# Gate and up projections of a hybrid decoder block: sixteen tiles as seven half-size matrix products

## Chip, cores and metric

One NeuronCore of a Trainium2 chip runs the whole program. The metric is device time in microseconds, the median of several runs; "span" is the time from the first to the last instruction in one profiled execution. TensorE is the matmul engine, VectorE, ScalarE and GpSimd are the three elementwise engines, SyncE only issues DMAs here.

## What is computed

The reference is one layer of a decoder block on x (1 x 512 x 1024, float32). Cut to what matters:

```
h = rms_norm(x, norm1); proj = h @ w_in
... differential attention (4 heads), native sparse attention (8 heads) ...
x = x + concat([o_diff, o_nsa]) @ w_out
h = rms_norm(x, norm2)
x = x + (silu(h @ w_gate) * (h @ w_up)) @ w_down        # w_gate, w_up: 1024 x 2816, w_down: 2816 x 1024
return rms_norm(x, final_norm)
```

## The kernel before

**Three matmuls for one.** Every float32 operand is split in two halves of fewer bits, high and low, and a product is the sum of high*high, high*low and low*high. A weight chunk (512 KB, 128 x 1024) goes through a ring: SyncE loads it into one of 3 `raw` slots, ScalarE rounds it to `w_hi` (one of 4 slots), and `w_lo` = `raw` - `w_hi` is made by GpSimd (`split`) for all chunks up to the down projection, and by VectorE (`split_down`) for those of the down projection. SyncE loads chunk k only when the low half of chunk k-3 is made; ScalarE makes the high half of chunk k only when TensorE is done with chunk k-4. Each queue works strictly in its written order.

**Stages.** Until about 312 us of the profiled execution: norm, input projection, attention and output projection, woven together by a written order of slots and jobs. There are 38 weight chunks in it; number 30 to 37 are those of the output projection (jobs `og` and `od`). The differential heads need each key half on both halves of the partitions: `double_keys` on GpSimd's queue copies them with four DMAs a head.

Then 22 tiles f of 128 hidden columns (`columns`): 24 matmuls of 512 columns for gate, 24 for up, on the un-normalised, transposed x (`xT_hi`, `xT_lo`: 8 blocks of 128 features by 512 tokens). VectorE takes each result from PSUM and multiplies it with the token's inverse norm `norm_b` (`gate_n`, `up_n`), ScalarE applies silu, VectorE multiplies. TensorE may start on a bank again when VectorE has taken it two tiles before (`s_gn`, `s_un`).

Last, the down projection as seven products of half matrices in place of eight (Strassen's method in Winograd's form, indices A11 to A22 and S1 to S4 for the token and feature halves and their sums, T1 to T4 for the weight sums). The seven combinations `form` of the hidden tiles are made by VectorE after every second tile. The four weight sums are made in DRAM: SyncE copies a piece (`down_sums`), and an accumulating DMA on GpSimd's queue (`add_sum`) adds the other; 24 such jobs of 256 to 512 KB, one behind each chunk from the fifth of gate and up on. A GpSimd job waits for its copy and for the accumulation four jobs before it, and the splits behind it in GpSimd's queue wait with it.

Of the kernel before, what the change touches and what calls it, by code (L numbers as in the profile page):

```python
# [25 lines left out]
P = 128  # L26
D = 1024
# [97 lines left out]

SUMS = [(T1, (0, 1), ("w", 0, 0)), (T3, (0, 1), ("w", 1, 1)), (T2, (0, 0), ("sum", T3)), (T4, (1, 0), ("sum", T2))]
SUM_AT = 4


def tiles_of(g):  # L130

    return 2 * g, min(2 * g + 2, FP)


def plan_chunks():
# [42 lines left out]
def hymba_block(nc, x, norm1, w_in, lambda_q1, lambda_k1, lambda_q2, lambda_k2, diff_subln,  # L178
# [8 lines left out]
    job_of = {c: j for j, c in enumerate(jobs)}  # L187

# [115 lines left out]
    with ExitStack() as ctx:  # L304
# [29 lines left out]
        with ExitStack() as compress:  # L334

            blk = [sb(f"blk{i}", [P, 16, 2, GROUPS * NC], F32R, compress) for i in range(2)]
        xres = sb("xres", [P, NT, D])
        with ExitStack() as second:

            high1 = sb("high1", [P, FP, HALF], F32R, second)  # L340
# [34 lines left out]
        with ExitStack() as swiglu:  # L375
            with ExitStack() as full:

                form = sb("form", [P, N_PROD, FP, HALF], F32, full)
            form_lo = sb("form_lo", [P, N_PROD, FP, HALF], F32R, swiglu)
            high0 = sb("high0", [P, FP, HALF], F32R, swiglu)  # L380
# [33 lines left out]
        s_last, s_gx = sem("s_last"), sem("s_gx")  # L414
        s_silu, s_prod, s_forms = sem("s_silu"), sem("s_prod"), sem("s_forms")
# [10 lines left out]
        HIGH = (high0, high1)  # L426
# [39 lines left out]
        def sum_job(i):  # L466

            to, begin, add = SUMS[i // GROUPS_M]
            return to, i % GROUPS_M, ("w",) + begin, add

        def sum_index(to, g):
            return [x_[0] for x_ in SUMS].index(to) * GROUPS_M + g

        def sum_done(eng, to, g):
            i = sum_index(to, g)
            eng.wait_ge(s_added[i % 4], 16 * (i // 4 + 1))

# [33 lines left out]
        def chunk_cols(k):  # L511
            if chunks[k][0] == "down":
                m0, m1 = tiles_of(chunks[k][1][1])
                return 512 * (m1 - m0)
            return SLOT if chunks[k][0] == "vg" else 1024

        def low_done(eng, k):

            if k >= down0:
                eng.wait_ge(s_dlo, k - down0 + 1)  # L520
            else:
                eng.wait_ge(s_split, k + 1)
# [14 lines left out]
        def _(sp):  # L537
# [9 lines left out]
            for k in range(len(chunks)):  # L547
# [11 lines left out]
                if chunks[k][0] == "vg":  # L559
# [5 lines left out]
                    sp.dma_start(dst[:, :, P:V_COLS], w[:, :, COL["vw"]:COL["gt"] + GATES]).then_inc(signal, 16)  # L565
# [1139 lines left out]
```

## Time and profile before

| what | value |
|---|---|
| median of 3 runs | 676.9 us (673.18 to 677.26) |
| the profiled execution | 673.63 us |
| its span | 671.8 us |
| granted TensorE clock, mean | 0.998 of full speed |
| TensorE matmul, busy | 659.1 us of the span |
| VectorE, ScalarE, GpSimd busy | 382.0, 321.9, 253.8 us |
| moved by DMA | 100.33 MB |

Busy matmul time overlaps from one matmul to the next, so its share says that TensorE has work, not at what rate; the rate is read from start to start. Waits are read per engine and per stage, since the stages have different limits.

### The profile page before, as it was taken

To read this page: it belongs to the slowest core of one execution; us is meant where nothing else is said; L and a number is where in the kernel's file an instruction comes from. 1 tells how busy PE (TensorE), PEld (TensorE's weight loads), DVE (VectorE), ACT (ScalarE), POOL (GpSimd) and SP (SyncE) were. 2 spreads that over 40 slices of the span, in tenths; PEclk is the share of its full clock that TensorE was granted. 3 is DMA by queue.
4 is the path that set the end of the run, shared out by engine and by line. 5 is a ranking of instruction groups with operands and counts; after the bars stand their busy time and mean duration, and the time that the engine had idled before them with its cause. 6 is when DMAs were issued, how large, how long until landed. Compare 5 with 4: busy or idle time off the path is not lost.

```text
span 671.8 us, 9932 instructions
## 1 busy us (share of the span) xinstructions
PE 659.1 (98%) x3483; PEld 558.8 (83%) x3483; DVE 382.0 (57%) x860; ACT 321.9 (48%) x658; POOL 253.8 (38%) x148
## 2 busy tenths in 40 slices
PE   9999999999999998999999999999999999999996
PEld 7988988898899887888788888888888888888884
DVE  6445356555665687523494466543444155778794
ACT  7546456688554477534432222222222224656663
POOL 4752242691212040222385576755444410000132
PEclk9999999999999999999999999999999999999999
DMA  8764341576222031223499999997333323766653
GB/s 252 201 141 125 88 120 49 153 188 215 54 59 63 17 80 16 63 64 95 156 230 296 277 267 282 302 271 176 94 101 96 107 80 128 204 179 198 186 172 127
DMA packets 103007, 100.33 MB, mean 149 GB/s; under 512 B 4036, under 2 KB 76848, under 8 KB 102960
## 3 DMA queue, kind: packets, MB, share of 16 engines
q1 hardware_dynamic: 93048, 83.23, 40.9%
q0 software_dynamic: 7776, 14.06, 11.7%
q10 hardware_dynamic: 2136, 2.43, 1.3%
q8 instruction: 28, 0.46, 0.3%
q14 instruction: 19, 0.16, 0.1%
HBM read 95.49 MB, written 27.54 MB: 183 GB/s over the span
## 4 chain that ended last, share of the span: by engine, by line
PE 93%; DVE 2%; issue 2%; POOL 1%; ACT 1%; POOLq 0%; DVEq 0%; ACTq 0%
PE bank L685 16%; PE bank L687 16%; PE bank L686 16%; PE bank L666 9%; PE bank L668 9%; PE bank L667 9%; PE bank L838 5%; PE bank L814 3%; PE bank L798 2%; PE bank L799 2%; PE bank L877 1%; PE bank L680 1%; POOL w_lo L619 1%; PE bank L832 1%; PE bank L851 1%
## 5 line engine op out<-in xcount | busy, mean ns | idle before, releaser
L619 POOL TENSOR_TENSOR w_lo<-raw,w_hi 128x1024 fp32r<-128x1024 f32 (+1 forms) x82 | 202.7, 2481 | 291.5 <-ACT w_hi L1006 290.8
L1006 ACT CAST w_hi<-raw 128x1024 fp32r<-128x1024 f32 (+2 forms) x123 | 125.4, 1025 | 202.9 <-PE bank L687 73.3
L685 PE MATMUL bank<-xT_hi,w_hi 128*128 128x512 f32 x464 | 184.0, 397 | 1.0 <-POOL w_lo L619 0.7
L687 PE MATMUL bank<-xT_hi,w_lo 128*128 128x512 f32 x464 | 182.4, 393 | 0.0
L686 PE MATMUL bank<-xT_lo,w_hi 128*128 128x512 f32 x464 | 182.0, 392 | 0.0
L687 PEld LDWEIGHTS bank<-xT_hi,w_lo 128*128 128x128 f32 x464 | 87.2, 188 | 19.7
L685 PEld LDWEIGHTS bank<-xT_hi,w_hi 128*128 128x128 f32 x464 | 87.3, 188 | 19.5 <-issue 1.1
L686 PEld LDWEIGHTS bank<-xT_lo,w_hi 128*128 128x128 f32 x464 | 87.4, 188 | 17.9 <-issue 0.2
L1431 DVE CUSTOM_DVE_ANT_0 bank<-bank,bias 128x128 f32<-128x128 f32 (+3 forms) x96 | 47.6, 497 | 75.8 <-PE bank L799 46.2
L668 PE MATMUL bank<-w_hi,form_lo 128*128 128x512 f32 x154 | 60.7, 394 | 0.0
L666 PE MATMUL bank<-w_hi,high 128*128 128x512 f32 x154 | 60.5, 393 | 0.0
L667 PE MATMUL bank<-w_lo,high 128*128 128x512 f32 x154 | 60.5, 393 | 0.0
L1087 ACT ACTIVATE E<-bank,nmax 128x128 f32<-128x128 f32 (+3 forms) x80 | 42.4, 531 | 35.7 <-DVE nmax L1431 34.8
L1588 DVE TENSOR_TENSOR w_lo<-raw,w_hi 128x1024 fp32r<-128x1024 f32 (+1 forms) x42 | 48.9, 1171 | 17.7 <-ACT w_hi L1006 17.4
L659 POOL TENSOR_TENSOR xres<-xres,final_g 128x512 f32<-128x512 f32 x7 | 13.0, 1879 | 111.5 <-ACT gate_n L1012 111.5
L1625 DVE TENSOR_TENSOR up_n<-bank,norm_b 128x512 f32<-128x512 f32 x22 | 15.1, 689 | 70.2 <-PE bank L687 70.2
L1099 ACT COPY PT<-bank 128x384 f32<-128x384 f32 (+3 forms) x84 | 35.4, 422 | 28.4 <-PE bank L814 28.0
L838 PEld LDWEIGHTS bank<-v_nsa,PT 128*128 128x128 f32 x320 | 43.5, 191 | 4.7 <-issue 1.6
L838 PE MATMUL bank<-v_nsa,PT 128*128 128x64 f32 x320 | 43.2, 266 | 0.3 <-DVE mix L1494 0.2
L814 PE MATMUL bank<-ident,E 128*128 128x128 f32 x208 | 36.8, 274 | 0.0
L1621 DVE TENSOR_TENSOR gate_n<-bank,norm_b 128x512 f32<-128x512 f32 x22 | 15.1, 688 | 35.4 <-PE bank L687 30.2
L667 PEld LDWEIGHTS bank<-w_lo,high 128*128 128x128 f32 x154 | 28.9, 188 | 6.7
(205 smaller groups left out, 1081.7 us busy)
## 6 DMA issues: line engine op xcount, KB each, us to landing
raw<-in_w_gate_dram SPq DMA_DIRECT2D x22, 512.0 KB, 8.1
raw<-in_w_up_dram SPq DMA_DIRECT2D x22, 512.0 KB, 6.8
raw<-in_w_in_dram SPq DMA_DIRECT2D x20, 512.0 KB, 4.3
down_sums<-in_w_down_dram SPq DMA_DIRECT2D x20, 512.0 KB, 12.4
raw<-down_sums SPq DMA_DIRECT2D x20, 512.0 KB, 3.8
raw<-in_w_down_dram SPq DMA_DIRECT2D x15, 512.0 KB, 3.5
down_sums<-in_w_down_dram POOLq DMA_DIRECT2D x10, 512.0 KB, 9.5
down_sums<-down_sums POOLq DMA_DIRECT2D x10, 512.0 KB, 8.9
```

Of the source, the lines that this page charges most:

```text
L619: nc.gpsimd.tensor_tensor(wv_lo(k)[:, 0:n], raw[:, k % RAW_SLOTS, 0:n], wv_hi(k)[:, 0:n].bitcast(F32), ALU.subtract).then_inc(s_split, 1)
L666: nc.tensor.matmul(o, a_hi, b_hi, start=first, stop=False)
L667: nc.tensor.matmul(o, a_hi, b_lo, start=False, stop=False)
L668: return nc.tensor.matmul(o, a_lo, b_hi, start=False, stop=last)
L685: nc.tensor.matmul(bank[:, :], hi, xT_hi[:, kt, :], start=kt == 0, stop=False)
L686: nc.tensor.matmul(bank[:, :], hi, xT_lo[:, kt, :], start=False, stop=False)
L687: return nc.tensor.matmul(bank[:, :], lo, xT_hi[:, kt, :], start=False, stop=kt == KT - 1)
L814: mm = nc.tensor.transpose(TURN[n % 2][:, j * P:(j + 1) * P], E[:, s % E_SLOTS, j * P:(j + 1) * P], ident[:, :])
L838: mm = nc.tensor.matmul(bank[:, 0:v.shape[1]], PT[:, n % 2, j * P:(j + 1) * P], v, start=j == 0, stop=j == i)
L1006: nc.scalar.copy(wv_hi(k)[:, 0:n], raw[:, k % RAW_SLOTS, 0:n]).then_inc(s_whi, 1)
L1431: nc.vector.tensor_tensor_reduce(out=bank[:, 0:n], in0=bank[:, 0:n], in1=bias[:, m % BIAS_SLOTS, 512 - n:512], scale=1.0, scalar=3.0e38, o ...
L1588: nc.vector.tensor_tensor(wv_lo(k)[:, 0:n], raw[:, k % RAW_SLOTS, 0:n], wv_hi(k)[:, 0:n].bitcast(F32), ALU.subtract).then_inc(s_dlo, 1)
```

## The change

The first six tiles (F0 = 6) stay as they are. For tiles 6 to 21 gate and up together are one 512 x 1024 times 1024 x 256 product: the token halves and the feature halves of x are the left side, gate's and up's columns, each with two feature halves, the right side. It is done as seven products of half matrices: a tile has 7 x 4 x 3 = 84 matmuls of 256 columns in place of 48 of 512. Its weights come in four chunks of 512, 512, 512 and 256 KB (`mixed`, c = 0 to 3), each of two loads of 256 KB (the last of one).

- The weight sums T1 to T4 of w_gate and w_up are made in DRAM (`mixed_sums`), in 32 more jobs of 512 KB copy and 512 KB accumulation. All 56 jobs are placed anew: ten behind chunks 6 to 15, ten behind 27 to 31, twelve behind 34 to 37, then twelve of the down sums behind the first twelve chunks of gate and up, and twelve behind every fifth of the mixed chunks.
- During tiles 0 to 5 VectorE also makes the normalised x (`normal_columns`: an addition of two SBUF tiles and a multiplication with PSUM for each of 8 blocks), four sums of its quarters (`x_sum`, 1024 columns) and the low halves of the seven left sides (`x_low`, 1024 columns); ScalarE makes their high halves (`x_high`).
- In the mixed tiles VectorE combines the seven results (seven additions of 256 columns, with ScalarE copying the first from PSUM), and VectorE, not GpSimd, makes the low halves of chunks c = 0 and 2. The product with silu of tile f-1 (`swiglu_tile`) stands in VectorE's order between the first addition of tile f and the low half of chunk (f+1, 0).
- The residual x is saved to DRAM after the output projection, since its space is taken, and loaded back in four pieces of 512 KB (`BACK`) in the down projection.
- `double_keys` has two DMAs a head in place of four.
- The down projection's six groups of tiles are 2, 2, 2, 1, 2, 2 in place of 2, 2, 2, 2, 2, 1.

```diff
+F0 = 6
+UNITS = [(A11, ("w", 0, 0)), (A12, ("w", 1, 0)), (S2, ("sum", T2)), (S3, ("sum", T3)),
+         (S1, ("sum", T1)), (A22, ("sum", T4)), (S4, ("w", 1, 1))]
+N_UNIT = 4
+X_ORDER = [A11, A12, S2, S3, A22, S1, S4]
+WIDE = 4
+BACK = {(0, 5): (0, 0), (1, 1): (0, 1), (1, 3): (1, 1), (2, 1): (1, 0)}
+X_FULL = {0: (0, 1, 2), 1: (3, 4, 5), 2: (6, 7)}
+X_SUMS = {2: (0, 1), 3: (2, 3)}
+X_SPLIT = {3: (A11, A12), 4: (S2, S3, A22), 5: (S1, S4)}
...
-    for f in range(FT):
+    for f in range(F0):
         chunks += [("gate", f), ("up", f)]
+    for f in range(F0, FT):
+        chunks += [("mixed", (f, c)) for c in range(N_UNIT)]
...
+    sum_at = [6 + i for i in range(10)] + [27 + i // 2 for i in range(10)] + [34 + i // 3 for i in range(12)]
+    sum_at += [n_fill + i for i in range(12)] + [n_fill + 2 * F0 + 2 + 5 * i for i in range(12)]
+    by_dve = [c[0] == "down" or (c[0] == "mixed" and c[1][1] in (0, 2)) for c in chunks]
...
-                    for z in range(2):
-                        k_ = k_diff[:, jobs[j][1] % 2, z, hd, :]
-                        pool.dma_start(k_[there, :], k_[here, :]).then_inc(s_dup[jobs[j][1]], 16)
+                    k_ = k_diff[:, jobs[j][1] % 2, :, hd, :]
+                    pool.dma_start(k_[there, :, :], k_[here, :, :]).then_inc(s_dup[jobs[j][1]], 16)
...
+            for f in range(F0, FT):
+                pe.wait_ge(s_un, f - 1)
+                for c in range(N_UNIT):
+                    k = index[("mixed", (f, c))]
+                    low_done(pe, k)
+                    for z, j in enumerate(units_of(c)):
+                        a = UNITS[j][0]
+                        if f == F0:
+                            pe.wait_ge(s_xlo, X_ORDER.index(a) + 1)
+                        o = SET[f % 2][c][:, HALF * z:HALF * z + HALF]
+                        for kt in range(4):
+                            w = slice(512 * z + P * kt, 512 * z + P * kt + P)
+                            nc.tensor.matmul(o, wv_hi(k)[:, w], x_hi(a)[:, kt, :], start=kt == 0, stop=False)
+                            nc.tensor.matmul(o, wv_hi(k)[:, w], x_lo(a)[:, kt, :], start=False, stop=False)
+                            mm = nc.tensor.matmul(o, wv_lo(k)[:, w], x_hi(a)[:, kt, :], start=False, stop=kt == 3)
+                    mm.then_inc(s_chunk, 1)
...
+            def normal_columns(kt):
+                x_ = x_full[:, kt, :]
+                link(nc.vector.tensor_tensor(x_, xT_hi[:, kt, :].bitcast(F32), xT_lo[:, kt, :].bitcast(F32), ALU.add))
+                nc.vector.tensor_tensor(x_, x_, NORM_BANK[:, :], ALU.mult).then_inc(s_xfull, 1)
...
+            for f in range(F0, FT):
+                first, second_, third, fourth = SET[f % 2]
...
+                dve.wait_ge(s_chunk, chunk[0])
+                dve.wait_ge(s_first, f - F0 + 1)
+                dve.wait_ge(s_prod, f - 1)
+                nc.vector.tensor_tensor(gate_[:, early], first_p, first[:, late_], ALU.add)
+                if f > F0:
+                    swiglu_tile(f - 1)
+                split_own(index[("mixed", (f, 0))] + SPLIT_SLOTS)
+                dve.wait_ge(s_chunk, chunk[1])
+                link(nc.vector.tensor_tensor(run_u, first_p, second_[:, early], ALU.add))
+                link(nc.vector.tensor_tensor(run_v, run_u, second_[:, late_], ALU.add))
+                split_own(index[("mixed", (f, 1))] + SPLIT_SLOTS)
+                dve.wait_ge(s_chunk, chunk[2])
+                dve.wait_ge(s_forms, f // 2)
+                nc.vector.tensor_tensor(gate_[:, late_], run_v, third[:, late_], ALU.add).then_inc(s_gn, 1)
+                nc.vector.tensor_tensor(up_[:, late_], third[:, early], run_v, ALU.subtract)
+                split_own(index[("mixed", (f, 2))] + SPLIT_SLOTS)
+                dve.wait_ge(s_chunk, chunk[3])
+                link(nc.vector.tensor_tensor(up_[:, early], fourth[:, early], run_u, ALU.subtract))
+                nc.vector.tensor_tensor(up_[:, early], up_[:, early], third[:, early], ALU.add).then_inc(s_un, 1)
+                split_own(index[("mixed", (f, 3))] + SPLIT_SLOTS)
+            swiglu_tile(FT - 1)
```

## Rows read from the trace of the kernel before

**Rows 1.** The page: busy time of the engines, and the chain that ended last

```profile
PE 659.1 (98%) x3483; PEld 558.8 (83%) x3483; DVE 382.0 (57%) x860; ACT 321.9 (48%) x658; POOL 253.8 (38%) x148
...
PE 93%; DVE 2%; issue 2%; POOL 1%; ACT 1%; POOLq 0%; DVEq 0%; ACTq 0%
```

**Rows 2.** Busy time by window, gate and up without sum jobs

```profile
470.00:555.00 85.00, 85.00 (x371) 69.45 (x370) 35.42 (x54) 22.61 (x28) 32.39 (x13) 1.00 0.33 98
```

**Rows 3.** Timeline of VectorE, up results of tiles 15 and 20: start, duration

```profile
492.62 0.69 DVE L1625 TENSOR_TENSOR up_n<-bank,norm_b 128x512 f32<-128x512 f32 x1 [4.77 <-PE bank L687]
...
547.86 0.69 DVE L1625 TENSOR_TENSOR up_n<-bank,norm_b 128x512 f32<-128x512 f32 x1 [4.77 <-PE bank L687]
```

**Rows 4.** Timeline of TensorE, 256 columns back to back, 22 starts apart

```profile
205.09 0.28 PE L667 MATMUL bank<-w_lo,xT_hi 128*128 128x256 f32 x1
...
207.71 0.28 PE L668 MATMUL bank<-w_hi,xT_lo 128*128 128x256 f32 x1
```

**Rows 5.** The page, costliest groups: halves of the weights

```profile
L619 POOL TENSOR_TENSOR w_lo<-raw,w_hi 128x1024 fp32r<-128x1024 f32 (+1 forms) x82 | 202.7, 2481 | 291.5 <-ACT w_hi L1006 290.8
L1006 ACT CAST w_hi<-raw 128x1024 fp32r<-128x1024 f32 (+2 forms) x123 | 125.4, 1025 | 202.9 <-PE bank L687 73.3
```

**Rows 6.** VectorE's groups by form, 470 to 555 us

```profile
L1636 DVE TENSOR_TENSOR form<-up_n,form 128x256 f32<-128x256 f32 x4 | 10.0, 2508 | 0.1
L1625 DVE TENSOR_TENSOR up_n<-bank,norm_b 128x512 f32<-128x512 f32 x8 | 5.5, 692 | 38.1 <-PE bank L687 38.1
...
L1588 DVE TENSOR_TENSOR w_lo<-raw,w_hi 128x1024 fp32r<-128x1024 f32 x2 | 2.4, 1217 | 0.0
...
L1638 DVE TENSOR_TENSOR form<-form 128x256 f32<-128x256 f32 x4 | 1.7, 417 | 0.0
```

**Rows 7.** Timeline of GpSimd at 493 us

```profile
493.81 2.57 POOL L619 TENSOR_TENSOR w_lo<-raw,w_hi 128x1024 fp32r<-128x1024 f32 x1 [3.05 <-ACT w_hi L1006]
```

**Rows 8.** Timeline of VectorE at 494 us

```profile
494.15 2.51 DVE L1636 TENSOR_TENSOR form<-up_n,form 128x256 f32<-128x256 f32 x1
```

**Rows 9.** Timeline of VectorE, tiles 0 and 1

```profile
333.13 0.69 DVE L1621 TENSOR_TENSOR gate_n<-bank,norm_b 128x512 f32<-128x512 f32 x1 [5.18 <-ACT norm_b L1213]
...
337.97 0.69 DVE L1625 TENSOR_TENSOR up_n<-bank,norm_b 128x512 f32<-128x512 f32 x1 [0.22 <-PE bank L687]
339.18 8.35 DVE L1633 TENSOR_TENSOR form<-gate_n,up_n 128x256 f32<-128x256 f32 x1 [0.51 <-ACT gate_n L1223]
```

**Rows 10.** Timeline of GpSimd, splits and sum jobs of the same time

```profile
337.25 2.88 POOL L619 TENSOR_TENSOR w_lo<-raw,w_hi 128x1024 fp32r<-128x1024 f32 x1
339.61 1.66 POOL L638 DMA_DIRECT2D down_sums<-in_w_down_dram  x1
...
343.48 3.76 POOL L619 TENSOR_TENSOR w_lo<-raw,w_hi 128x1024 fp32r<-128x1024 f32 x1
```

**Rows 11.** DMA, 470 to 555 us, no sum jobs: share of 16 engines, us to landing

```profile
q1 hardware_dynamic: 12706, 8.30, 32.4%
...
raw<-in_w_gate_dram SPq DMA_DIRECT2D x5, 512.0 KB, 3.9
```

**Rows 12.** DMA issues, 345 to 450 us, a sum job behind each load

```profile
down_sums<-in_w_down_dram SPq DMA_DIRECT2D x15, 512.0 KB, 12.5
raw<-in_w_gate_dram SPq DMA_DIRECT2D x10, 512.0 KB, 11.6
```

**Rows 13.** DMA issues, 320 to 345 us, where the sum jobs begin

```profile
raw<-in_w_up_dram SPq DMA_DIRECT2D x3, 512.0 KB, 4.3
raw<-in_w_gate_dram SPq DMA_DIRECT2D x2, 512.0 KB, 7.1
```

**Rows 14.** Timeline of GpSimd, output projection: splits of chunks 36 and 37

```profile
289.09 4.77 POOL L619 TENSOR_TENSOR w_lo<-raw,w_hi 128x1024 fp32r<-128x1024 f32 x2 [8.40 <-ACT w_hi L1006]
```

**Rows 15.** Timeline of TensorE: first use of chunk 37

```profile
302.37 0.40 PE L666 MATMUL bank<-w_hi,mixT 128*128 128x512 f32 x1
```

**Rows 16.** Timeline of TensorE: the matmul behind the key-doubling DMAs at 129 us

```profile
129.40 0.47 PE L685 MATMUL bank<-xT_hi,w_hi 128*128 128x512 f32 x1 [0.72 <-POOL w_lo L619]
```

More of the change, by code:

```diff
@@ L464, in part, with mixed_part, sum_part, sum_done @@
             return w[:, m0:m1, rows_, 512 * dh:512 * dh + 512]
[L466 to L475, printed above, removed]
+        def mixed_part(what, f0, n, k0=0, n_k=4):
+            if what[0] == "sum":
+                w = mixed_sums[what[1]].rearrange("(k p) n -> p k n", p=P)
+                return w[:, k0:k0 + n_k, P * (f0 - F0):P * (f0 - F0 + n)]
+            rows_, up = what[1:]
+            w = (w_up if up else w_gate)[0].rearrange("(k p) n -> p k n", p=P)
+            return w[:, 4 * rows_ + k0:4 * rows_ + k0 + n_k, P * f0:P * (f0 + n)]
+        def sum_part(i, what):
+            kind, _, at_, _, _ = todo[i]
+            if kind == "down":
+                return part(what, at_[0])
+            return mixed_part(what, F0 + WIDE * at_[0], WIDE, 2 * at_[1], 2)
+        def sum_done(eng, kind, to, at_):
+            i = [x_[:3] for x_ in todo].index((kind, to, at_))
             eng.wait_ge(s_added[i % 4], 16 * (i // 4 + 1))
+        def units_of(c):
+            return range(2 * c, min(2 * c + 2, len(UNITS)))
         def chunk_src(k):
@@ L514, in chunk_cols @@
                 return 512 * (m1 - m0)
+            if chunks[k][0] == "mixed":
+                return 512 * len(units_of(chunks[k][1][1]))
             return SLOT if chunks[k][0] == "vg" else 1024
         def low_done(eng, k):
[L519 to L522, printed above, removed]
+            eng.wait_ge(s_dlo if by_dve[k] else s_split, sum(by_dve[m] == by_dve[k] for m in range(k + 1)))
         SHARE = OUTP[(len(turned) - 1) % 2][:, 256:512]
@@ L588, in _ @@
                 sp.wait_ge(s_y, t + 1)
[L589 removed]
+                sp.dma_start(out[0, t * P:(t + 1) * P, 0:c], xlast[:, t, 0:c]).then_inc(s_out, 16)
             sp.wait_ge(s_out, 16 * (NT + 1))
@@ L599, in raw_landed @@
         def raw_landed(eng, k):
-            loads = sum(2 if chunks[m][0] == "vg" else 1 for m in range(k % RAW_SLOTS, k + 1, RAW_SLOTS))
+            loads = sum(2 if chunks[m][0] == "vg" or chunks[m][0] == "mixed" and len(units_of(chunks[m][1][1])) > 1 else 1
+                        for m in range(k % RAW_SLOTS, k + 1, RAW_SLOTS))
             eng.wait_ge(s_raw[k % RAW_SLOTS], 16 * loads)
@@ L1618, in _, with split_own @@
+            def split_own(k):
+                if k < len(chunks) and by_dve[k]:
+                    split_down(k)
+            for f in range(F0):
                 dve.wait_ge(s_chunk, late(("gate", f)))
```

247 lines of the change are left out of this document (182 added, 65 removed).

## The prediction

> **What bounds the kernel now.** I read the page first: TensorE is busy for 659.1 of 671.8 us and holds 93% of the chain that ended last [rows 1]. Then the windows: between 470 and 555 us it is busy all 85 us, at the higher of its two clock levels (granted clock 1.00, 2.4 GHz), while VectorE is busy 35 and GpSimd 32 us [rows 2]. So gate and up are bound by the number of matmuls times their spacing. The spacing I take from starts: the up results of tiles 15 and 20 are fetched 55.24 us apart, so a tile takes 11.05 us, and with 48 matmuls that is 0.230 us each [rows 3]. The duration printed for a matmul is of no use here, since neighbours overlap.
>
> **What the change removes.** 84 matmuls of 256 columns replace 48 of 512. The same shape stands back to back in the attention part: 22 intervals in 2.62 us, 0.1191 us each, at the full clock, with another weight block before each, as in the new loop [rows 4]. A mixed tile is then 84 x 0.1191 = 10.00 us, 1.05 less than before. Sixteen tiles: **16.7 us** is what there is to gain, 2.5% of the span. (Half the width costs 0.52 of the full one, so seven eighths of the columns become 0.905 of the time.) All else that the change does must hide behind TensorE, and for each I name the cover.
>
> **Weights through the ring.** A tile's weights grow from 1 MB in 11.05 us to 1.75 MB in 10.0 us. A raw slot sees all four kinds of chunk in three tiles. Outside the load it is held for three whole and one half high parts (3 x 1.03 + 0.6 = 3.7 us), and for the low parts: two by VectorE at 1.22, one and a half by GpSimd at 2.48, together 6.2 us [rows 5, 6]. With a load time L that is (4L + 9.9)/3 per tile. With L = 3.9 us, as without sum jobs [rows 11], it gives 8.5 us, below TensorE's 10.0. It reaches 10.0 us at L = 5.0, and the old 11.05 at L = 5.8. What L will be is open: without other traffic 1 MB in 11.05 us took 32.4% of the DMA engines [rows 11], so 1.75 MB in 10.0 us take about 0.63. One sum job follows every fifth chunk, every 12.5 us; before there was one every 5.5 us, and L was 11.6 [rows 12]. Where the jobs began, loads took 4.3, and those caught with a copy 7.1 us [rows 13]. If two in five are caught, L is 5.4 on average, but a chunk is needed only when TensorE has used up what is split: four high and low slots, 10 us of work, so that one late load is absorbed. Bounds: nothing, to (4 x 5.8 + 9.9)/3 = 11.05, the whole gain. I take 1 us, near the lower end, because the late ones come singly.
>
> **VectorE against GpSimd.** This is where I expect most of the loss. A VectorE operation on two SBUF tiles takes 0.417 us at 256 columns, and the same operation directly behind the start of a GpSimd split takes 2.51 us [rows 6, 8]. The split runs from 493.81 to 496.38, the VectorE operation ends at 496.66 [rows 7, 8]: it waited for the split to end. Results from PSUM (0.692 us for 512 columns) don't show it [rows 6]. At tile 1, with GpSimd at splits and sum jobs one after another, a single operation took 8.35 us [rows 9, 10]. Before, VectorE had time for that. Now there are two places where it has not.
>
> First, **tiles 0 to 5**. VectorE starts at 333.8 us with the new work [rows 9]. On two SBUF tiles: 8 additions of 512 columns (0.68 each, between 0.417 and 1.217), four sums and seven low halves of 1024 (11 x 1.22), 27 products and combinations of 256 (0.417 each), two low halves of weights (1.22 each) [rows 6], 32.6 us in all. From PSUM: 8 multiplications and 12 results, 20 x 0.69 = 13.8 us. GpSimd makes nine and a half low parts in that time, 23.6 us [rows 5]. If all PSUM work runs under GpSimd's, S1's low half is ready 32.6 + 23.6 - 1.2 = 55.0 us after 333.8, at 388.8; if none does, at 402.6. TensorE wants it two chunks into tile 6: tile 1 ends at 337.9 [rows 9], four more tiles to 382.1, and 48 matmuls, 387.8 us. So this costs between 1 and 15 us, once. I take 6: about two thirds of the PSUM work finds a split to run under.
>
> Second, **the mixed tiles**. TensorE can't begin tile f+1 before VectorE has made the low half of chunk (f+1, 0), whose slot is free when chunk (f, 0) is done. From then: ScalarE's high half 1.05, its copy of the first result and VectorE's first addition 0.4 each, `swiglu_tile`, the low half 1.22 us. With an even f-1 `swiglu_tile` has two operations, 0.8 us, and all is done after some 4.1 us. With an odd f-1 it has seven, 2.9 us: 6.2 us with the handovers. TensorE has three chunks, 60 x 0.1191 = 7.15 us of cover. But GpSimd begins (f+1, 1) after 2.86 + 1.05 + 0.1 = 4.0 us, in the midst of the seven, and holds VectorE back until 6.5: the low half is there after 8.4 us, and TensorE waits 1.2 us. Every second tile, 8 x 1.2 = 9.6 us at most. It is nothing where GpSimd's chunk lands 0.6 us later, since then VectorE's low half is under way first. I take half, 5 us.
>
> **Attention and output projection.** 32 sum jobs lie here. SyncE and GpSimd wait in them, and the splits behind wait too. In the attention part low halves are made long before use. The tight place is twelve jobs behind chunks 34 to 37. The splits of 36 and 37 ended at 293.9 [rows 14]. Chunk 37 is first used at 302.4 us [rows 15], so it has 8.5 us of cover. Two jobs in front of it wait for sums four or eight jobs earlier, each some 9 to 12 us from issue to landing under load (the copy took 12.5, [rows 12]); laid out one after the other this puts its split at about 301.5. It costs 0 to 3 us; I take 0.5. The two fewer key DMAs a head can give at most what TensorE waited behind that queue, 0.72 us at 129 us [rows 16]; I take 0.5. The save and reload of the residual, four loads of 512 KB in the down projection, each come three or more chunks before use: 0, unless the ring there, now with 14% more loads, runs late. The changed groups: 0.
>
> **Sum.** 16.7 + 0.5 - 6 - 5 - 1 - 0.5 = 4.7 us. On the profiled execution (673.6 us, span and 1.8 around it) that is 668.9. The median of the runs is 3.3 us higher, so on the median's footing **672 us**.
>
> **The rivals.**
> (a) All is hidden. For it: in the old trace TensorE never waits in this stage, and where VectorE lags the queues shift by themselves until the collisions stop. Then 16.7 + 0.7 less the 1 us that can't be avoided: 660 us.
> (b) VectorE sets the pace of the mixed tiles. Its work a tile is seven combinations (2.9), two low halves (2.4) and on average 4.5 operations of `swiglu_tile` (1.9), 7.3 us, and GpSimd's 3.7 us beside it; if they exclude each other wholly, 11.0 us a tile, and the gain is gone while the 6 us before tile 6 stay: 682 us. Against it: the seven combinations read PSUM.
> (c) Slower: the weight ring. If one load in four takes 11.6 us, as under steady sum jobs, and the others 4.3 [rows 12, 13], L is 6.1 and a tile takes 11.4 us; 0.35 x 16 = 5.7 us lost, plus 6 before tile 6: 688 us. It decides from L = 5.8 on. For it: every such load passes through SyncE's one queue with the copies. Against it: a sum job only every 12.5 us.
> (d) Half the columns don't give half the time. The rows give 0.1191 against 0.230 us [rows 3, 4], so 0.01. The Trainium skill, "TensorE: Matmul & The Clock Gate", section "Back-to-back issue gap", states about 81 ns for 128 and 131 ns for 512 columns in a sustained stream; read between the two, 256 columns would cost some 98 ns, 84 of them 8.2 us against 6.3 us for 48 of the old, and the change would lose 1.9 us a tile by that estimate, about 707 us. This case's trace doesn't agree with either figure: its 512 columns stand 230 ns apart.
>
> The other place where a page bears on it: the Trainium skill, "DMA: Bandwidth & Descriptors", section "Measured (HBM→SBUF, 128 partitions, SWDGE, issued from GpSimd)", advises transfers of 1 MiB and more and lists 138 GB/s at 64 KB and 341 GB/s at 1 MB, and the change cuts its loads from 512 to 256 KB. By it each load would be less efficient, which pushes towards (c). The two of a chunk follow each other in one queue, so I count them as one of 512 KB.
>
> **Chances.** The forecast (most of the gain eaten by waits, 665 to 679) 0.46, (a) 0.22, (b) 0.16, (c) 0.15, (d) 0.01. A measurement tells about 1% here, 6.8 us. Below 670.1 lie (a) and four tenths of the forecast: 0.41. Within lie the rest of it and half of (b): 0.35. Above 683.7 the rest, 0.24. The range of 8 in 10 takes in (a) nearly whole and (b), and about half of (c): 661 to 687 us.
>
> **What the new profile would show.** Matmuls of 256 columns 0.119 us apart inside a chunk. A wait of TensorE for `x_lo` or for the low half before the third chunk of tile 6, with VectorE operations of 0.4 to 1.2 us stretched to 3 before it. From tile 7 on a wait of about 1 us before the first matmul of every second tile, put down to VectorE's `w_lo`. Loads of 256 KB in the mixed stage with a median under 5 us; if TensorE's waits there are put down to GpSimd's low halves, and ScalarE's to the loads, (c) is right. A wait at the output projection's last chunk of up to 3 us. The prediction is wrong on the fast side if VectorE's operations stretch less than here because GpSimd has less to do, and on the slow side if loads stay above 5.8 us.

## The result, and the profile after

The changed kernel takes **727.1 us** (median of 4 runs, 725.9 to 728.9) against 676.7 us of before: ratio 1.076, 95% interval [1.072, 1.080]. I had forecast 672 us, 661 to 687. The page of the profiled execution (728.9 us, span 727.1):

```profile
PE 662.8 (91%) x4059; PEld 589.4 (81%) x4059; DVE 455.2 (63%) x999; ACT 357.9 (49%) x713; POOL 272.6 (37%) x172
...
q1 hardware_dynamic: 128696, 114.69, 51.4%
q0 software_dynamic: 16352, 30.84, 24.4%
...
PE 47%; DMA 19%; issue 13%; POOL 9%; DVE 7%; ACT 3%; SPq 1%; POOLq 0%; DVEq 0%; ACTq 0%
```

TensorE has only 3.7 us more busy time than before, but its share of the chain that ended last fell from 93% [rows 1] to 47%; DMA transfers hold 19%. Three marks of the timelines say where the 55.3 us of span went. VectorE's first use of `norm_b` comes at 358.65 us, 25.5 later than before [rows 9]. Tile 5 ends 25.9 us later than before (408.0 against 382.1), so tiles 0 to 5 lose hardly more. The mixed stage then lasts from 408.0 to 614.0 us, 206 us where sixteen old tiles took 16 x 11.05 = 176.8 [rows 3]: 29.2 more. What follows is as long as before, within 0.3 us.

```profile
358.65 0.69 DVE L1835 TENSOR_TENSOR gate_n<-bank,norm_b 128x512 f32<-128x512 f32 x1 [3.96 <-ACT norm_b L1346]
```

**Loss 1, 25.5 us before `norm_b`.** TensorE's waits in the output projection and behind it, and busy time by window (TensorE's is the second number; behind the engines stand the granted clock, the DMA engines' share and GB/s):

```profile
302.83 0.49 PE L781 MATMUL bank<-w_hi,mixT 128*128 128x512 f32 x1 [3.33 <-POOL w_lo L733]
335.62 0.79 PE L800 MATMUL bank<-xT_hi,w_hi 128*128 128x512 f32 x1 [12.57 <-DVE xT_lo L1490]
```

```profile
300.00:320.00 20.00, 17.17 (x76) 14.15 (x77) 5.42 (x8) 4.31 (x10) 11.36 (x9) 0.91 1.11 219
320.00:340.00 20.00, 7.43 (x24) 5.63 (x23) 3.92 (x6) 5.31 (x11) 7.54 (x5) 0.68 1.05 250
```

The first wait, 3.33 us, is for the low half of chunk 36. GpSimd's rows show its split and that of chunk 37, and TensorE's row the first use of chunk 37, which came just in time:

```profile
299.88 2.80 POOL L733 TENSOR_TENSOR w_lo<-raw,w_hi 128x1024 fp32r<-128x1024 f32 x1
...
309.55 2.85 POOL L733 TENSOR_TENSOR w_lo<-raw,w_hi 128x1024 fp32r<-128x1024 f32 x1
```

```profile
312.82 0.39 PE L781 MATMUL bank<-w_hi,mixT 128*128 128x512 f32 x1
```

Chunk 37 is used 10.5 us later than before [rows 15], ahead of the large wait. Of these, 3.8 us are there by 282.8 us, behind a wait for the key copies at 256.6. The profiled execution of **keys** below, which has no job more than the kernel before, is 3.1 us late at the same place, and that of **nomix** is not; so this part comes and goes between executions, and the jobs aren't shown to be its cause.

The sixteen DMA engines are full. The wait of 12.57 us is put down to VectorE's `xT_lo`, but that waited for ScalarE, and ScalarE for a load. ScalarE's row and SyncE's queue (start, time that the issue took) show why:

```profile
331.18 1.04 ACT L1139 CAST w_hi<-raw 128x1024 fp32r<-128x1024 f32 x1 [15.37 <-DMA raw<-in_w_up_dram]
```

```profile
302.71 0.37 SPq L677 DMA_DIRECT2D raw<-in_w_up_dram  x1
303.12 11.50 SPq L682 DMA_DIRECT2D down_sums<-in_w_down_dram  x1
314.67 2.77 SPq L677 DMA_DIRECT2D raw<-in_w_gate_dram  x1
317.48 14.48 SPq L682 DMA_DIRECT2D down_sums<-in_w_down_dram  x1
```

The load of chunk 39 (tile 0's `up`), issued at 302.71, landed at about 331, 28 us later. A copy for the sums kept SyncE for 11.50 and 14.48 us in the issue alone, with the next load behind it. ScalarE makes high halves in the order of the ring, so tile 0's late `up` weights held back the residual's high columns, which TensorE needed first.

**Loss 2, 29.2 us in the mixed stage, where 16.7 were to be gained.** The half-width matmuls are as forecast, 22 intervals in 2.64 us inside tile 6, 0.120 us each [rows 4]; then the waits begin:

```profile
408.10 0.28 PE L1097 MATMUL bank<-xa,w_hi 128*128 128x256 f32 x1
...
410.74 0.29 PE L1098 MATMUL bank<-xa,w_lo 128*128 128x256 f32 x1
...
421.86 0.55 PE L1096 MATMUL bank<-xs,w_hi 128*128 128x256 f32 x1 [6.11 <-DVE xs L1802]
422.21 0.41 PE L1097 MATMUL bank<-xs,w_hi 128*128 128x256 f32 x1
422.42 0.41 PE L1098 MATMUL bank<-xs,w_lo 128*128 128x256 f32 x1
```

Before tile 6's sums TensorE waits 7.7 us in all (1.64 and 6.11), and right behind the second wait the starts stand 0.21 us apart in place of 0.12, at the lower of the two clock levels; the window from 422 to 426 us (the clock is third from the end) has it at half:

```profile
422.00:426.00 4.00, 4.00 (x19) 4.00 (x20) 4.00 (x3) 0.00 (x0) 1.94 (x1) 0.50 0.01 2
```

Waits and lower clock together make tile 6 20.1 us long, 10.1 more than its 84 x 0.119. From there on, the list of waits between 425 and 610 us (in total, times, longest), and VectorE's first addition of each mixed tile (shortest, median, longest ns; first and last start):

```profile
DVE gate_n L1857 <- ACT sq L1387: 58.7, 14, 6.6
ACT w_hi L1139 <- DMA raw<-mixed_sums: 38.7, 26, 4.5
...
PE bank L1096 <- DVE w_lo L1753: 25.1, 11, 6.6
```

```profile
L1857 DVE TENSOR_TENSOR gate_n<-sq,bank x16: 406/421/424, 424.9 to 608.5; 128x256 f32<-128x256 f32 x16
```

Fifteen tiles in 183.6 us, **12.24 us a tile**. TensorE's own starts, from tile 7 to the first matmul of the down projection, give 12.40: 36.0 us over fifteen times 10.0, of which 25.1 are the waits above and some 8 are lost by matmuls that start 0.21 us apart behind them, at the lower clock. TensorE waits for VectorE's low halves, VectorE for ScalarE's copy of the first result (58.7 us in 14 times), and ScalarE, which rounds the next tile's first chunk ahead of that copy, for its load. The loads of 256 KB from the sums had a median of 4.8 us, those from `w_gate` 3.9. A chunk is two such loads (the last of a tile one); from the issue of its first to the landing of its last it took 5.35 us on the mean of all mixed chunks from tile 7 on.

### The profile page after: what moved, and what is told of

The parts are those of the page before. It is cut to its first block, busy times and chain, and to the rows that moved or that the text cites. A ratio compares the mean times of both kernels' runs of the same rounds, so it can differ in the third digit from the quotient of the medians.

```text
span 727.1 us, 11548 instructions
## 1 busy us (share of the span) xinstructions
PE 662.8 (91%) x4059; PEld 589.4 (81%) x4059; DVE 455.2 (63%) x999; ACT 357.9 (49%) x713; POOL 272.6 (37%) x172
## 3 DMA queue, kind: packets, MB, share of 16 engines
q1 hardware_dynamic: 128696, 114.69, 51.4%
q0 software_dynamic: 16352, 30.84, 24.4%
## 4 chain that ended last, share of the span: by engine, by line
PE 47%; DMA 19%; issue 13%; POOL 9%; DVE 7%; ACT 3%; SPq 1%; POOLq 0%; DVEq 0%; ACTq 0%
POOL w_lo L733 7%; PE bank L781 6%; PE bank L783 6%; PE bank L782 6%; DMA down_sums<-in_w_down_dram 6%; PE bank L953 4%; DMA raw<-mixed_sums 4%; DMA raw<-in_w_gate_dram 4%; PE bank L800 4%; PE bank L802 3%; PE bank L801 3%; PE bank L929 2%; DMA mixed_sums<-in_w_up_dram 2%; PE bank L913 2%; DVE w_lo L1753 2%
## 5 line engine op out<-in xcount | busy, mean ns | idle before, releaser
L1139 ACT CAST w_hi<-raw 128x1024 fp32r<-128x1024 f32 (+1 forms) x155 | 151.9, 985 | 201.4 <-DMA raw<-in_w_up_dram 63.5
L1753 DVE TENSOR_TENSOR w_lo<-raw,w_hi 128x1024 fp32r<-128x1024 f32 x74 | 90.2, 1219 | 25.5 <-ACT w_hi L1139 25.3
L800 PE MATMUL bank<-xT_hi,w_hi 128*128 128x512 f32 x208 | 84.8, 408 | 13.5 <-DVE xT_lo L1490 12.8
L802 PE MATMUL bank<-xT_hi,w_lo 128*128 128x512 f32 x208 | 82.7, 397 | 0.0
L801 PE MATMUL bank<-xT_lo,w_hi 128*128 128x512 f32 x208 | 82.6, 397 | 0.0
L1096 PE MATMUL bank<-xs,w_hi 128*128 128x256 f32 x256 | 73.6, 288 | 8.3 <-DVE xs L1802 7.7
L1097 PE MATMUL bank<-xs,w_hi 128*128 128x256 f32 x256 | 73.2, 286 | 0.0
L1098 PE MATMUL bank<-xs,w_lo 128*128 128x256 f32 x256 | 73.1, 286 | 0.0
L1096 PEld LDWEIGHTS bank<-xs,w_hi 128*128 128x128 f32 x256 | 49.9, 195 | 8.8 <-issue 8.1
L774 POOL TENSOR_TENSOR xlast<-xlast,final_g 128x512 f32<-128x512 f32 x7 | 12.8, 1851 | 101.1 <-ACT gate_n L1145 101.1
L1097 PEld LDWEIGHTS bank<-xs,w_hi 128*128 128x128 f32 x256 | 49.7, 194 | 0.0
L1098 PEld LDWEIGHTS bank<-xs,w_lo 128*128 128x128 f32 x256 | 49.6, 194 | 0.0
L802 PEld LDWEIGHTS bank<-xT_hi,w_lo 128*128 128x128 f32 x208 | 39.6, 191 | 9.2
L1857 DVE TENSOR_TENSOR gate_n<-sq,bank 128x256 f32<-128x256 f32 x16 | 6.7, 420 | 63.5 <-ACT sq L1387 58.7
## 6 DMA issues: line engine op xcount, KB each, us to landing
mixed_sums<-mixed_sums POOLq DMA_DIRECT2D x16, 512.0 KB, 12.4
```

The costliest lines, as they stand in the source:

```text
L800: nc.tensor.matmul(bank[:, :], hi, xT_hi[:, kt, :], start=kt == 0, stop=False)
L801: nc.tensor.matmul(bank[:, :], hi, xT_lo[:, kt, :], start=False, stop=False)
L802: return nc.tensor.matmul(bank[:, :], lo, xT_hi[:, kt, :], start=False, stop=kt == KT - 1)
L1096: nc.tensor.matmul(o, wv_hi(k)[:, w], x_hi(a)[:, kt, :], start=kt == 0, stop=False)
L1097: nc.tensor.matmul(o, wv_hi(k)[:, w], x_lo(a)[:, kt, :], start=False, stop=False)
L1098: mm = nc.tensor.matmul(o, wv_lo(k)[:, w], x_hi(a)[:, kt, :], start=False, stop=kt == 3)
```

## The experiments

Two theories. **A:** the sum jobs (a copy and an accumulate, DRAM to DRAM, 512 KB each) fill the DMA engines; loads come late. **B:** in the mixed tile the copy of the first result stands behind a load on ScalarE, which closes a loop. The main rival is that VectorE, slowed by GpSimd, or the order of the ring sets the pace whatever the loads take. Every time below is a median, and its ratio is to runs of the kernel before on the same chip (674.7 to 677.1 us there). The kernels named nomix leave the weight sums of gate and up out and load plain weights in their place, and those named nodown do the same with the twelve late down sums, so they compute another output.

**keys.** The key DMAs alone, in the kernel before: one DMA for both parts, `s_dup` at 32 in place of 64.

> The kernel before with two key-doubling DMAs a head in place of four, nothing else. Every theory: between 0 and 0.7 us faster than before, no change that a measurement tells; none of the 50 us comes from here.

674.4 us, 0.997 [0.995, 1.000]. TensorE's wait of 0.72 us at 129 us [rows 16] is now 0.5. The sign is right; the size, 2.7 us between the medians, is at the edge of what can be measured and more than this wait can give.

**nomix.** Theory A alone.

```diff
-    for wide in range(0, (FT - F0) // WIDE, 2):
+    for wide in ():
-  mixed_part(UNITS[j][1], f, 1)
+  mixed_part(("w", 0, 0) if UNITS[j][1][0] == "sum" else UNITS[j][1], f, 1)
```

> The changed kernel without its 32 jobs that make the weight sums of gate and up in DRAM (the loads of those sums take a piece of the gate weights in their place, so the results are not the reference's). Theory A (the early loss is the DMA engines filled with the twelve jobs behind chunks 34 to 37): the 25.9 us before tile 0's results are gone, norm_b is reached by 333 to 335 us, and the mixed stage stays at 12.9 us a tile: 699 to 704 us. Rival (GpSimd's waits in its own queue or ScalarE's order, not the engines' load, or the save of the residual): most of the 25.9 us stays, 720 us.

702.3 us, 1.039 [1.036, 1.041]; `norm_b` is used at 332.2 us. Loss 1 is gone, all of it, with the save of the residual still in place, so theory A holds for that stretch. The price of a job: the two large DMA queues' shares are 51.4 + 24.4% of 727.1 us after and 45.7 + 11.7% of 700.0 here, so 32 jobs took (551.1 - 401.8)/32 = **4.7 us of all sixteen engines each**. This is the time of their packets as the view counts it, which also gave windows shares of 1.11, so it is a price under load and no lower bound. The mixed tile is unchanged:

```profile
L1853 DVE TENSOR_TENSOR gate_n<-sq,bank x16: 407/421/422, 397.9 to 581.5; 128x256 f32<-128x256 f32 x16
```

**spread** and **spread_first.** The twelve jobs of chunks 34 to 37 go behind 32 and 33, the down jobs four chunks later; the second kernel also turns ScalarE's order round.

```diff
-    ... + [34 + i // 3 for i in range(12)]
+    ... + [32] * 4 + [33] * 8
```

```diff
 for c in range(N_UNIT):
-    weights_hi(index[("mixed", (f, c))] + SPLIT_SLOTS)
     if c == 0:
+        act.wait_ge(s_chunk, late(("mixed", (f, 0))))
         act.wait_ge(s_gn, f)
         nc.scalar.copy(first_p, SET[f % 2][0][:, 0:HALF]).then_inc(s_first, 1)
+    weights_hi(index[("mixed", (f, c))] + SPLIT_SLOTS)
```

> The changed kernel, all jobs kept, with the last twelve mixed jobs four behind chunk 32 and eight behind chunk 33 (where DMA engines and GpSimd are idle before 276 us) and the down jobs four chunks later, as the kernel before had them. Theory A: the jobs are done before the output projection's last chunks are loaded, and the time is as without the jobs, 699 to 706 us. Rival (it is the number of jobs and the load they put on the attention part, wherever they stand): no better than 720 us.

> As the kernel with the jobs moved, and in the mixed tiles ScalarE copies the first result out of PSUM before it makes the next high half, not behind it. Theory B (the mixed stage loses by order: VectorE's seven operations and the low half behind them stand behind ScalarE's copy, which stands behind a high half that waits for its load): VectorE's operations move into the time of the load, TensorE's 25 us of waits for the low half fall by half or more, 8 to 20 us faster than with the jobs moved alone. Theory C (the ring itself: load, high, low and the next load take longer than three chunks of TensorE, whatever the order): 0 to 4 us faster.

spread: 739.9 us, 1.093 [1.089, 1.098], a miss. GpSimd's and TensorE's rows:

```profile
270.01 1.14 POOL L751 DMA_DIRECT2D mixed_sums<-mixed_sums  x1 [2.31 <-DMA mixed_sums<-mixed_sums]
270.69 1.67 POOL L741 DMA_DIRECT2D k_diff<-k_diff  x2
```

```profile
281.31 0.45 PE L913 MATMUL bank<-k_diff,q_diff 128*128 128x128 f32 x1 [26.49 <-issue]
```

The last head's key DMAs were issued behind eight accumulates and took up to 9.9 us to land, the second at 281.2, and TensorE stood 26.5 us for those keys. spread_first: 718.0 us, 1.062 [1.059, 1.065]. Theory B holds, 22 us against spread (18 between the two profiled executions).

**first.** The changed kernel with ScalarE's order turned round and nothing else.

> The changed kernel, with one thing exchanged on ScalarE: in each of the sixteen mixed tiles it first copies the finished first product out of its bank, and then rounds the weights of the next tile's first chunk (before: the other way round, so that the copy stood behind a load that had not landed). Theory B (the stage lost its time to the copy behind a late load, which stopped VectorE, which holds the chunk that the next load waits for): the same 20 to 24 us as between the two kernels with their jobs elsewhere (739.9 and 718.0), so 703 to 707; VectorE's waits for ScalarE's copy fall from 58.7 us to under 10, the mixed stage takes about 11.7 us a tile. Rival (what was gained there belonged to the other place of the sum jobs): within 5 us of 727.

716.3 us, 1.058 [1.056, 1.061]: 10.8 us gained, half of what was expected, though VectorE's wait for the copy fell from 58.7 to 5.0 us and the tile to 11.15 us. Part of the contrast is in which executions are compared: between the profiled ones this pair differs by 14.7 us and the spread pair by 18.2. The order costs time here too; how much of the 22 us belonged to the other places of the jobs stays open.

**nomix_first**, **nomix_nodown**, **nomix_first_nodown.** With nomix these are the four corners: order of the copy, and the twelve down jobs inside the mixed stage. The second edit:

```diff
-    return todo
+    return todo[:-12]
-    sum_at = ... + [n_fill + 2 * F0 + 2 + 5 * i for i in range(12)]
+    sum_at = [n_fill + i for i in range(12)]
```

> Both known losses taken away: the 32 sum jobs of gate and up are left out (their loads read 256 KB of the gate weights in their place, so the output is another), and ScalarE copies the first result before it rounds the next weights. Theory (the two losses are independent and add up): 702.3 less 22 = 680, norm_b used at 332, 11.6 us a mixed tile. Rival (without the jobs the DMA engines are less full, so that the loads come sooner and the ring no longer sets the tile): 10.0 to 10.6 us a tile, 655 to 665.

> As the run without the 32 sum jobs of gate and up and with the copy of the first result first (688.7 us, 11.5 us a mixed tile), and also without the twelve jobs of the down sums that were issued inside the mixed stage (the loads of those sums read down weights in their place). Theory (the ring paces the tile by full DMA engines: 1.84 MB of weights a tile are 6.3 us of all sixteen at some 290 GB/s, and three quarters of a job at 4.5 us are 3.4 more, 9.7 of the 10.0 that TensorE needs): without them the median load falls from 5.3 to under 4.3 us and the tile to 10.0 to 10.4 us, 667 to 672. Rival (the order of work on ScalarE, VectorE and GpSimd in the ring sets it, whatever the loads take): 11.2 us a tile or more, 684 to 689.

> The changed kernel with its own order on ScalarE (the next tile's weights rounded ahead of the copy of the first result), without the 32 sum jobs of gate and up and without the twelve of the down sums inside the mixed stage (their loads read plain weights, so the output is another). With the copy first the same kernel took 666.6 us, 9.81 us a mixed tile. Theory (the order costs only because the loads come late behind full DMA engines): the loads land in time here, within 3 us of 666.6, 9.8 to 10.0 us a tile. Rival (the order is a cause of its own): 11 us a tile or more, 683 or more.

Without the 32 jobs, in us. A tile is given between VectorE's first additions, and by TensorE's starts from tile 7 on; a load as the median of one of 256 KB, and as the mean of a chunk from first issue to last landing:

```
                                  copy behind the load           copy first
12 jobs   time (ratio to before)  702.3 (1.039 [1.036, 1.041])   688.7 (1.019 [1.016, 1.023])
          a tile, both ways       12.24, 12.41                   11.50, 11.69
          one load; a chunk       4.8; 5.4                       5.3; 5.9
no job    time (ratio to before)  690.7 (1.024 [1.020, 1.027])   666.6 (0.988 [0.985, 0.991])
          a tile, both ways       11.37, 11.38                   9.81, 10.00
          one load; a chunk       3.9; 4.3                       4.3; 4.6
```

Each cause alone costs about two thirds of what both cost. nomix_first took 9 us more than its theory had (two losses that add up) and 24 more than the upper end of its rival; nomix_first_nodown is where its theory put it. With the jobs gone and the copy first, TensorE is busy 140 of 140 us; this is the stage as it was meant:

```profile
400.00:540.00 140.00, 140.00 (x1179) 140.00 (x1178) 101.38 (x191) 66.10 (x90) 54.60 (x27) 1.00 0.66 184
```

TensorE's first matmuls of tiles 8 and 21 stand thirteen tiles and 130.00 us apart, 10.00 us a tile:

```profile
411.03 0.28 PE L1094 MATMUL bank<-xa,w_hi 128*128 128x256 f32 x1
...
541.03 0.28 PE L1094 MATMUL bank<-xa,w_hi 128*128 128x256 f32 x1
```

The 9.81 from the additions is too low as a pace of TensorE: VectorE's first addition of tile 6 comes late, behind the entry, and the later ones catch up.

VectorE's additions of the two copy-first kernels, without and with the twelve jobs, and the issues of each between 400 and 550 us:

```profile
L1856 DVE TENSOR_TENSOR gate_n<-sq,bank x16: 407/421/422, 398.3 to 545.5; 128x256 f32<-128x256 f32 x16
```

```profile
q1 hardware_dynamic: 53070, 27.51, 64.9%
...
raw<-in_w_gate_dram SPq DMA_DIRECT2D x84, 256.0 KB, 4.3
```

```profile
L1854 DVE TENSOR_TENSOR gate_n<-sq,bank x16: 408/416/422, 398.5 to 571.0; 128x256 f32<-128x256 f32 x16
```

```profile
q1 hardware_dynamic: 49035, 27.85, 65.0%
q0 software_dynamic: 2464, 4.72, 19.2%
...
raw<-in_w_gate_dram SPq DMA_DIRECT2D x78, 256.0 KB, 5.3
```

A median load 1.0 us longer, or 1.3 us a chunk, costs 1.7 us a tile: the ring has no slack at 5.3. nomix_nodown refutes what I expected of it (that the order is harmless where loads are in time). Its loop, in ScalarE's, VectorE's and SyncE's rows:

```profile
474.47 1.05 ACT L1137 CAST w_hi<-raw 128x1024 fp32r<-128x1024 f32 x1 [0.68 <-DMA raw<-in_w_gate_dram]
475.43 0.36 ACT L1385 COPY sq<-bank 128x256 f32<-128x256 f32 x1
```

```profile
463.09 0.42 DVE L1855 TENSOR_TENSOR gate_n<-sq,bank 128x256 f32<-128x256 f32 x1 [3.27 <-ACT sq L1385]
...
465.81 2.61 DVE L1757 TENSOR_TENSOR form_lo_a<-form_a,high_a 128x256 fp32r<-128x256 f32 x1
468.34 1.21 DVE L1751 TENSOR_TENSOR w_lo<-raw,w_hi 128x1024 fp32r<-128x1024 f32 x1
...
471.05 1.21 DVE L1751 TENSOR_TENSOR w_lo<-raw,w_hi 128x1024 fp32r<-128x1024 f32 x1
...
475.88 0.42 DVE L1855 TENSOR_TENSOR gate_n<-sq,bank 128x256 f32<-128x256 f32 x1 [2.83 <-ACT sq L1385]
```

```profile
469.58 0.37 SPq L667 DMA_DIRECT2D raw<-in_w_up_dram  x1
469.99 5.57 SPq L667 DMA_DIRECT2D raw<-in_w_gate_dram  x6
```

Read it as a circle. The addition at 463.09 starts VectorE on the work of two tiles; the low half at the end of it (468.34) frees the raw slot for which SyncE's next load stands (469.58), and the load of the chunk that matters is behind it in SyncE's queue (469.99); it lands, ScalarE rounds it at 474.47, and only then copies (475.43), for which VectorE's next addition has waited 2.83 us (475.88). Once round is 12.4 to 12.9 us, and 9.6 to 11.1 in the tiles with less VectorE work (from tile 8 on). With the copy first, VectorE runs ahead of the load and the circle is open.

**nomix_first_rows.** Is it the bytes or the 512-byte rows? The loads read 2048-byte rows of `w_down`.

> As the run without the 32 jobs and with the copy first, but all seven 256 KB loads of a mixed tile read pieces of w_down whose rows are 2048 bytes in one piece for each partition, in place of four rows of 512 bytes (other weights, so the output is another). It asks whether the weight ring (time from issue to landing) sets the 11.6 us a tile that are left. If it does: the median load falls from about 4.5 to about 3 us, the tile to 10.0 to 10.4 us (what TensorE needs), 655 to 660. If VectorE or the order of ScalarE's work sets it: within 4 us of the run with short rows, with the loads faster for nothing.

685.2 us, 1.014 [1.010, 1.017]: 3.4 us better than with short rows, the median load 4.7 in place of 5.3, the tile 11.23. The packets fell from 55,008 to 17,854 between 400 and 570 us and the loads' share of the engines only from 64.3 to 59.1%. The gain is small against the intervals of the two ratios. So the length of the rows is not what fills the engines here, bytes count for most, and the forecast of 10.0 to 10.4 us a tile is missed.

**nomix_first_nodown_early.** `X_SPLIT` one tile earlier: `{3: (A11, A12, S2), 4: (S3, A22, S1), 5: (S4,)}`.

> As the run without the 44 jobs, with the splits of the input sums one plain tile earlier (S2 behind tile 3, S1 behind tile 4, S4 alone behind tile 5), which changes only the entry to tile 6. Theory (the entry wait of 7.8 us for the input's low halves is VectorE's work piled up behind tile 5, and drops TensorE to its half clock behind it): the wait falls under 3 us and the time by 4 to 7 us against the same kernel without it. Rival (VectorE is as full in the plain tiles, so that the work only moves): within 2 us of it.

667.2 us, 0.990 [0.986, 0.993], the same as without. TensorE's wait for `xs` fell from 6.1 to 1.1 us, and waits of 5.2 us for VectorE's `w_lo` came up. The rival holds: VectorE's work only moved from one wait to another.

**placed_first**, **placed2_first**, **placed3_first.** The whole change with the copy first, the key DMAs ahead of the jobs at each chunk, and the jobs at other places.

```diff
 placed_first
+    [6 .. 15] + [17, 19, 21, 26] + [27 + i // 3 for i in range(18)]
 placed2_first
+    [6 .. 15] + [17, 19, 21, 23, 25, 26] + [27 + i // 2 for i in range(10)] + [32, 33, 34, 35, 36, 37]
 placed3_first, down jobs
+    [n_fill + i, i < 12] + [n_fill + 12 + 9 * i, i < 6] + [down0 + 2 + 4 * i, i < 6]
```

> The whole change, nothing left out, with the copy of the first result ahead of the weights, and the 32 sum jobs of gate and up placed behind chunks 6 to 15, 17, 19, 21, 26 and 27 to 32 (three each), so that none stands behind chunk 33 or later; at each chunk GpSimd issues the two key copies of a head before its sum jobs; the down sums' jobs of the six plain tiles come four chunks later. Theory (the stall of 26.7 us in the kernel with twelve jobs behind chunks 32 and 33 was TensorE waiting for the last head's keys behind eight jobs in GpSimd's queue, and the DMA engines have room before 280 us): no wait of TensorE over 4 us between 230 and 340 us, norm_b used at 333 to 338, total 718 less 24 = 692 to 697. Rival (the DMA engines are full there whatever the order; each job costs 4.5 us of all sixteen, so a stall of 10 to 25 us only moves): 705 to 718.

> The whole change, nothing left out, with the copy of the first result first and the two key copies ahead of the sum jobs of a chunk; the 32 jobs of gate and up spread as evenly as the chunks allow: behind chunks 6 to 15, 17, 19, 21, 23, 25, 26, two each behind 27 to 31, one each behind 32 to 37. Theory (with three jobs a chunk at 27 to 32 the DMA engines were full from 140 to 270 us and 17 us went in waits for late loads; each job is 4.5 us of all sixteen, there is room for 32 only if no stretch gets more than it has free): norm_b used at 335 to 345 in place of 350, 690 to 700. Rival (the room is not there: wherever they go, some 15 us are lost): 702 to 712.

> The whole change, nothing left out, as the kernel with the 32 jobs spread evenly (699.0 us, norm_b at 342.5, 11.55 us a mixed tile), but of the twelve late jobs of the down sums only the six of T2 stay in the mixed stage; the six of T4, which only the last product reads, stand in the down stage, one behind every fourth chunk, where the DMA engines are busy 0.56 to 0.73 of the time; the twelve early ones come four chunks sooner. Theory (the mixed tile goes from 9.8 us with no job to 11.55 with twelve in proportion): 10.6 to 10.8 us a tile, 684 to 688. Rival (the loads of the sums and of the weights alone already fill the ring once anything is beside them): 11.3 us a tile or more, 695 or more; or the six jobs delay the down loads, and the stage from the first down product on takes over 118 us in place of 113.

placed_first: 705.3 us, 1.041 [1.038, 1.045]; `norm_b` at 350.1, so the rival's case: DMA engines at shares of 0.96 to 1.09 in every window from 140 to 260 us, and TensorE idle inside. Two of its windows:

```profile
140.00:160.00 20.00, 16.85 (x103) 14.95 (x102) 9.71 (x33) 14.87 (x30) 13.88 (x7) 0.91 0.96 256
...
220.00:240.00 20.00, 15.97 (x95) 13.53 (x95) 10.59 (x48) 8.83 (x29) 8.06 (x6) 0.91 1.06 254
```

placed2_first: 699.0 us, 1.036 [1.033, 1.039]; `norm_b` at 342.5, as expected, 11.55 us a tile. placed3_first: 697.6 us, 1.033 [1.029, 1.037], which misses the 684 to 688. Its tile did come down, to 10.37 us, further than forecast, and the mixed stage is 12.5 us shorter than in placed2_first. Of that 1.3 us are lost again before `norm_b` and 8.0 in the down stage (121.0 us from its first product on, against 113.0), where the six moved jobs stand beside the loads of the ring and the residual's reload, so the second of its rivals is the one that came:

```profile
L1860 DVE TENSOR_TENSOR gate_n<-sq,bank x16: 408/416/422, 410.5 to 566.0; 128x256 f32<-128x256 f32 x16
```

```profile
580.00:600.00 20.00, 17.11 (x72) 12.97 (x70) 9.70 (x14) 8.39 (x12) 1.14 (x1) 1.00 1.00 333
```

No placement that I tried of the whole work beats the kernel before. What is left of the gap is open in one point: whether another placement would reach the 666.6 us of the kernel without the 44 jobs. The three tried suggest that jobs pushed out of one stretch are paid for in another.

## Why the prediction was wrong, step by step

- **Half-width matmuls, 16.7 us.** Right. 0.120 us in tile 6; in the stage with neither the jobs nor the loop TensorE takes 10.00 us a tile, 0.119 for each of 84, the forecast's numbers. Rival (d) is out. The estimate from the Trainium skill's page "TensorE: Matmul & The Clock Gate" (some 98 ns) is below all of these.
- **Attention and output projection, 0 to 3 us, taken 0.5.** This is the first step that failed: 25.5 us. I added up the latencies of two jobs in GpSimd's queue (9 to 12 us) and compared them with chunk 37's cover of 8.5 us. Even this sum was short: chunk 37's split ended at 312.4 us, where I had 301.5, and only because TensorE was late already (3.33 us of it for chunk 36) did it not wait for chunk 37. Above all I did not add up the engines' time. All twelve accumulations behind chunks 34 to 37 and three of their twelve copies were issued between 282 and 320 us, with the first jobs of the down sums and the loads of the ring beside them. From 282 to 336 us the queue of the accumulations (q0) and that of the copies and loads (q1) took, as shares of all sixteen engines:

```profile
q0 software_dynamic: 3536, 6.82, 71.2%
q1 hardware_dynamic: 5420, 5.37, 35.0%
```

The cover that ended was that of a load behind, two chunks on (39), with the residual's high columns behind it on ScalarE: 12.57 us in one wait.
- **Weights through the ring, 1 us.** The second that failed, in two ways. The formula, (4L + 9.9)/3, has L for a whole chunk, and a chunk took 5.35 us on the mean (the median of single loads, 4.8, is not that L, though it fulfils the mark "under 5 us"). That gives 10.4 us a tile; the tile took 12.4. The formula lacks ScalarE's copy in the order of the ring: I named that copy among the handovers of tile f+1, but with the load taken as landed, and never closed the circle. With the copy first the formula is nearly right: 5.9 us a chunk give 11.1, and 11.69 was measured (nomix_first); 4.6 give 9.5, below TensorE's 10.00, and 10.00 was measured (nomix_first_nodown). So the late load that I took as absorbed, one at a time, wasn't: the cost of the stage's twelve jobs is 22 us with the copy first (688.7 against 666.6), where I counted 1.
- **VectorE against GpSimd in the mixed tiles, 5 us.** I expected most of the loss here, and this step failed too, as a cause of its own. The stretching is there (2.61 us at 465.81, under the GpSimd split of 465.59) but its own price is nothing: with the loads in time and the copy first TensorE didn't wait once between 400 and 540 us. The sign that I named for it did come, a wait for VectorE's `w_lo` at the start of about every second tile, 1.5 to 6.6 us long, but it was the circle's. Inside the circle the stretching lengthens the round (2.61 us in place of 0.42 in the round shown); how much of the 12.8 us is its doing wasn't tried apart.
- **Tiles 0 to 5 and the entry to tile 6, 6 us.** Right in place and cause: 7.7 us, 6.11 and 1.64, for `xs` from VectorE. What I left out is that the wait is followed by matmuls at the lower clock, here and behind the long waits of the later tiles; with it tile 6 lost 10.1 us.
- **Key DMAs, 0.5 us.** As measured in sign; the 2.7 us between the medians of keys can't tell its size.
- **Rival (c)** had the sign, and the queue; but by its own condition (L over 5.8) it would not have decided in the changed kernel, since a chunk took 5.35 on the mean. Rival (b) is refuted by the 10.00 us.
- **The Trainium skill's page "DMA: Bandwidth & Descriptors"**, section "Measured (HBM→SBUF, 128 partitions, SWDGE, issued from GpSimd)", prefers large transfers. Loads of 256 KB took 3.9 us in nomix_nodown, as long as those of 512 KB before without sum jobs [rows 11], which points the same way, though with shorter rows and other traffic around them.

The sum that would have been right, on the profiled executions: 16.7 for the matmuls, less 25.9 before tile 6 (forecast 0.5), 10.1 in tile 6 (forecast 6) and 36.0 in tiles 7 to 21 (forecast 5 and 1), is the 55.3 us that were lost. For the kernel without the 44 jobs it is 16.7, less 1 before tile 6 and 7.9 in tile 6: some 8 us, which the medians give too. The jobs and the copy's order then cost 60 (727.1 against 666.6). That the forecast had the entry's term about right is no more than that; the loss came from the two terms that it had put next to nothing.

## What to carry to other kernels

DRAM-to-DRAM work put "beside" a kernel has to be paid from the DMA engines' free time: take each job's engine time (here 4.7 us of all sixteen for 512 KB copied and accumulated, measured under load), add it up per stretch, and compare it with what the windows show as free, before looking at any latency. In a prefetch ring follow each buffer once round, through every engine's program order: an operation that a consumer waits for must not stand behind one that waits for the consumer's own release. Take the load time of a ring from the first issue to the last landing of what fills a slot, as a mean, and a stage's pace from the starts of the engine that bounds it. Here an arithmetic saving of 12% of one stage's columns was worth 2.5% of the kernel, and is lost as soon as its operands must be fetched or made at the pace of a full queue.

## What the runs showed of the hardware

- Two issues on SyncE's queue stood for 11.5 and 14.5 us while the DMA engines' share was 1.11 and 1.05, and the loads behind them weren't even issued.
- With the engines full a load of 512 KB took 28 us from issue to landing, against 3.9 without sum jobs [rows 11].
- Behind a wait of 6.11 us TensorE's granted clock was 0.50 from 422 to 426 us, and matmuls of 256 columns started 0.21 us apart in place of 0.12.
- Two causes that act on the same ring don't add: 24.1 us (the order) and 22.1 us (the jobs) alone, 35.7 together.
